# The gates stage of a diffusion trunk: a third hi/lo weight buffer, and every lo part on VectorE

## The reference

```python
def peer_ffn(h, w_q, keys, u_tab, v_tab):
    q = (h @ w_q)...                                   # 8 heads, two halves of 128
    s = jnp.einsum('bthcd,hckd->bthck', q, keys)       # 128 keys a half
    s_top, i_top = lax.top_k(s, PEER_TOPK)             # 16 of each half
    ...
    best_s, pos = lax.top_k(cand_s, PEER_TOPK)         # 16 of the 256 pairs
    idx = jnp.take_along_axis(cand_i, pos, axis=-1)    # experts out of 128 * 128
    gates = jax.nn.softmax(best_s, axis=-1)
    ...
    pre = jnp.einsum('ced,cd->ce', jnp.take(u_tab, ii, axis=0), hh)
    act = jax.nn.gelu(pre)
    return jnp.einsum('ce,ced->cd', act * gg, jnp.take(v_tab, ii, axis=0))
```

## Time and profile before

| | us |
|---|---|
| median of 3 runs | 4571.91 (4570.05 to 4576.68) |
| the profiled execution | 4570.1 |
| its span, first to last instruction | 4568.4 |
| gates stage, layer 0 | about 736 to 1616 of the span |
| gates stage, layer 1 | about 3279 to 3969 of the span |
| TensorE busy | 4062.0 (89%) |
| VectorE busy | 3121.7 (68%) |
| ScalarE busy | 1898.0 (42%) |
| GpSimd busy | 1492.6 (33%) |

### The profile page before, as it was taken

One profiled execution on the slowest core, in us unless ns is written; L12 is line 12 of the kernel. 1 busy time (PEld: TensorE's weight loads), 2 busy tenths in 40 slices (PEclk: granted clock), 3 DMA queues, 4 the chain that ended last, 5 costly groups with the idle time before them and its releaser, 6 DMA issues. The chain is left out here.

```text
span 4568.4 us, 62858 instructions
## 1 busy us (share of the span) xinstructions
PE 4062.0 (89%) x20380; PEld 3461.7 (76%) x20380; DVE 3121.7 (68%) x5714; ACT 1898.0 (42%) x3664; POOL 1492.6 (33%) x1048
## 2 busy tenths in 40 slices
PE   8687697899999989999978889867799999899998
PEld 2576586778888868888856767645699999899997
DVE  0675378998887668888874454534887765477777
ACT  1211222577777722222223333322257777533332
POOL 0122123555554434444412111102354444322221
PEclk9798898999999999999998898878899999899999
DMA  6333113799999999999941010011278888799996
GB/s 249 130 139 110 41 43 107 244 326 324 330 329 327 343 345 375 373 375 372 374 165 60 33 37 28 28 37 65 75 246 294 282 275 292 261 333 331 336 330 221
DMA packets 411875, 1025.96 MB, mean 225 GB/s; under 512 B 33968, under 2 KB 182448, under 8 KB 405680
## 3 DMA queue, kind: packets, MB, share of 16 engines
q1 hardware_dynamic: 301104, 621.00, 38.7%
q0 software_dynamic: 110592, 402.70, 24.6%
HBM read 904.03 MB, written 119.54 MB: 224 GB/s over the span
## 5 line engine op out<-in xcount | busy, mean ns | idle before, releaser
L156 PE MATMUL psum<-h_hi,w_hi 128*128 128x512 f32 (+1 forms) x2880 | 1140.1, 396 | 309.9 <-POOL w_lo L133 294.5
L129 ACT ACTIVATE w_hi<-w_raw 128x1024 fp32r<-128x1024 f32 x624 | 660.5, 1059 | 1471.1 <-PE psum L1215 863.0
L133 POOL TENSOR_TENSOR w_lo<-w_raw,w_hi 128x1024 fp32r<-128x1024 f32 x258 | 640.7, 2484 | 1471.2 <-ACT w_hi L129 1469.1
L157 PE MATMUL psum<-h_lo,w_hi 128*128 128x512 f32 (+1 forms) x2880 | 1095.4, 380 | 0.0
L158 PE MATMUL psum<-h_hi,w_lo 128*128 128x512 f32 (+1 forms) x2880 | 1094.9, 380 | 0.0
L156 PEld LDWEIGHTS psum<-h_hi,w_hi 128*128 128x128 f32 x2880 | 560.5, 195 | 396.1 <-POOL w_lo L133 188.6
L133 DVE TENSOR_TENSOR w_lo<-w_raw,w_hi 128x1024 fp32r<-128x1024 f32 x366 | 448.4, 1225 | 537.4 <-ACT w_hi L129 513.0
L1213 PE MATMUL psum<-a_hie,w_hi 128*128 128x512 f32 (+1 forms) x2048 | 758.9, 371 | 34.5 <-DVE a_loe L1266 34.5
L1214 PE MATMUL psum<-a_loe,w_hi 128*128 128x512 f32 (+1 forms) x2048 | 756.9, 370 | 0.0
L1215 PE MATMUL psum<-a_hie,w_lo 128*128 128x512 f32 (+1 forms) x2048 | 749.2, 366 | 0.0
L1198 POOL DMA_INDIRECT v_rowse<-in_peer_v,expert_idx x384 | 423.6, 1103 | 825.9 <-DVE row_sume L1275 812.8
(11 more groups left out here) (200 smaller groups left out, 4437.9 us busy)
## 6 DMA issues: line engine op xcount, KB each, us to landing
w_raw<-in_peer_u SPq DMA_DIRECT2D x256, 512.0 KB
w_raw<-in_peer_v SPq DMA_DIRECT2D x256, 512.0 KB
gates<-stageg SPq DMA_DIRECT2D x28, 2048.0 KB
acts<-act_gg SPq DMA_DIRECT2D x128, 256.0 KB
gte<-gates SPq DMA_DIRECT2D x32, 1024.0 KB
act_fe<-acts SPq DMA_DIRECT2D x128, 256.0 KB
ada_w<-in_ada_w SPq DMA_DIRECT2D x12, 2048.0 KB, 7.7
ada_rows<-in_ada_w SPq DMA_DIRECT2D x48, 512.0 KB, 3.5
```

The source lines that it names most:

```text
L129: act.activation(self.w_hi[:, s, :], self.raw[:, slot, :], ACT.Copy).then_inc(self.hi_done, 1)
L133: pool.tensor_tensor(self.w_lo[:, s, :], self.raw[:, slot, :], self.w_hi[:, s, :].bitcast(F32), ALU.subtract).then_inc(self.lo_done, 1)
L156: pe.matmul(out, wh, hi[:, k], start=(k == 0), stop=False)
L157: pe.matmul(out, wh, lo[:, k], start=False, stop=False)
```

## The change

The gates stage gets a third pair of hi and lo buffers, kept in a list `more` that only this stage fills. `W` = 3 is their number there, and tile c uses buffer c % 3. ScalarE makes the hi part of tile c+3 after product c, where it made that of tile c+2. VectorE makes all lo parts, tiles 0 and 1 before its first selection and then that of tile c+2 as it comes to tile c; GpSimd is left with the gathers. Room for the buffers comes from the gathered rows (`UBUF` 5 to 4) and the one-hots (`EQ` 3 to 2). The accumulators stay two, the raw slots four, and SP's loop isn't edited. GpSimd's list places each gather three tiles later than before, relative to the tiles that it no longer touches.

```diff
--- before.py
+++ after.py
@@ -44,7 +44,7 @@
 GROUPS = NKEYS // QUAD
 SPARSE = (2, 1)
 LEAD = (16, 20)
-UBUF = 5
+UBUF = 4
 VBUF = (8, 4)
 
 
@@ -96,6 +96,7 @@
         self.settled = sem("settled")
         self.tiles = 0
         self.wide = 2
+        self.more = []
 
     def sem(self, name):
 
@@ -119,19 +120,25 @@
         eng.sem_inc(self.settled, 1)
 
 
+    def weights(self, x):
+
+        if x < SPLIT:
+            return self.w_hi[:, x, :], self.w_lo[:, x, :]
+        return self.more[x - SPLIT]
+
     def load(self, sp, src, i, slot, n_raw, turn):
         sp.wait_ge(self.lo_done, i + (self.tiles + RAW - n_raw + 1))
         sp.dma_start(self.raw[:, slot, :], src).then_inc(self.raw_in[slot], 16)
 
     def hi(self, act, i, slot, s, turn):
         act.wait_ge(self.raw_in[slot], turn * 16 + (self.raw_at[slot] + 16))
-        act.wait_ge(self.tile_done, i + (self.tiles + 1))
-        act.activation(self.w_hi[:, s, :], self.raw[:, slot, :], ACT.Copy).then_inc(self.hi_done, 1)
+        act.wait_ge(self.tile_done, i + (self.tiles + 1 - len(self.more)))
+        act.activation(self.weights(s)[0], self.raw[:, slot, :], ACT.Copy).then_inc(self.hi_done, 1)
 
     def lo(self, pool, i, slot, s):
         pool.wait_ge(self.hi_done, i + (self.tiles + 1))
-        pool.tensor_tensor(self.w_lo[:, s, :], self.raw[:, slot, :], self.w_hi[:, s, :].bitcast(F32),
-                           ALU.subtract).then_inc(self.lo_done, 1)
+        hi, lo = self.weights(s)
+        pool.tensor_tensor(lo, self.raw[:, slot, :], hi.bitcast(F32), ALU.subtract).then_inc(self.lo_done, 1)
 
     def context_h(self, scope, tag):
 
@@ -143,14 +150,13 @@
         x = [(self.h_hi[:, :, 0:min(tokens, SEQ)], self.h_lo[:, :, 0:min(tokens, SEQ)])]
         return x + ([(self.hc_hi[:], self.hc_lo[:])] if tokens == TOK else [])
 
-    def product(self, pe, i, s, moving, ks=range(KC)):
+    def product(self, pe, i, s, moving, ks=range(KC), w=None):
 
         if ks[0] == 0:
             pe.wait_ge(self.lo_done, i + (self.tiles + RAW + 1))
             pe.wait_ge(self.acc_free[s], i // 2 + (self.tiles // 2 + 1))
         for k in ks:
-            wh = self.w_hi[:, s, k * P:(k + 1) * P]
-            wl = self.w_lo[:, s, k * P:(k + 1) * P]
+            wh, wl = (x[:, k * P:(k + 1) * P] for x in self.weights(s if w is None else w))
             for n, (hi, lo) in enumerate(moving):
                 out = self.psum[:, self.wide * s + n, 0:hi.shape[2]]
                 pe.matmul(out, wh, hi[:, k], start=(k == 0), stop=False)
@@ -773,7 +779,7 @@
     tag = f"g{layer}"
     K = TOPK
     STAGES, STAGE_G = P // STAGE_T, STAGE_T // 4
-    EQ, OJ = 3, 2
+    EQ, OJ, W = 2, 2, SPLIT + 1
     dots = S * P
     moving = t.moving(Td)
     t.wide = 1
@@ -797,6 +803,7 @@
         act_f = sb("act_g", [P, 2, Td])
         ubuf = sb("u_rows", [P, UBUF, D])
         pre_act = sb("pre_act", [P, S, P])
+        t.more = [(sb("w_hi", [P, D], F32R)[:], sb("w_lo", [P, D], F32R)[:])]
         h_row = t.psum[:, 2:4, :]
         gelu_done = t.sem("gelu_done" + tag)
         spilled = [t.sem(f"spilled{x}{tag}") for x in range(2)]
@@ -832,7 +839,7 @@
         turn_h = [next(p for p in range(END) if dots_by(p) >= P * s) for s in range(1, S)]
 
         def on_pool(c):
-            return c < lead or c % 2
+            return c < 0
 
         with nc.Block() as block:
 
@@ -848,9 +855,10 @@
                     dve.wait_ge(dv, steps[0])
 
                 def low(c):
+
                     if c < NKEYS and not on_pool(c):
                         dve.wait_ge(t.lo_done, c + (t.tiles + RAW))
-                        t.lo(dve, c, c % RAW, c % SPLIT)
+                        t.lo(dve, c, c % RAW, c % W)
 
                 def dots_to(upto):
 
@@ -893,7 +901,7 @@
                     while here[0] < min(upto, END):
                         p = here[0]
                         if p % KC == 0:
-                            low(p // KC + 1)
+                            low(p // KC + 2)
                         if p + 14 in group_at:
                             one_hots(group_at[p + 14])
                         if p % 2:
@@ -947,6 +955,8 @@
                         between()
                     return sparse
 
+                low(0)
+                low(1)
                 for n, (end, sparse, b) in enumerate(order):
                     begin, calls = here[0], [0]
 
@@ -1003,7 +1013,7 @@
                             turn(turn_at[p])
                         if p in group_at:
                             group(group_at[p])
-                        t.product(pe, c, c % SPLIT, moving, [k])
+                        t.product(pe, c, c % SPLIT, moving, [k], c % W)
 
             @block.scalar
             def _(act):
@@ -1014,8 +1024,8 @@
                 def ahead(c):
 
                     t.wait_product(act, c)
-                    if c + SPLIT < NKEYS:
-                        t.hi(act, c + SPLIT, (c + SPLIT) % RAW, c % SPLIT, (c + SPLIT) // RAW)
+                    if c + W < NKEYS:
+                        t.hi(act, c + W, (c + W) % RAW, c % W, (c + W) // RAW)
                     act.wait_ge(spilled[c % 2], 16 * (c // 2 + 1))
                     act.activation(act_f[:, c % 2], t.acc(c % SPLIT, Td), ACT.Gelu).then_inc(gelu_done, 1)
                     act.wait_ge(gelu_done, c + 1)
@@ -1051,7 +1061,7 @@
                         act.wait_ge(u_used, s * P)
                     act.activation(h_row, h_tok[:, s].rearrange("p (b n) -> p b n", b=2),
                                    ACT.Copy).then_inc(h_ready, 1)
-                for i in range(SPLIT):
+                for i in range(W):
                     t.hi(act, i, i, i, 0)
                 h_copy(0)
                 ends = [0] + [end for end, _, _ in order]
@@ -1081,8 +1091,8 @@
                 for c in range(NKEYS):
                     if on_pool(c):
                         pool.wait_ge(t.lo_done, c + (t.tiles + RAW))
-                        t.lo(pool, c, c % RAW, c % SPLIT)
-                    upto = dots if c == NKEYS - 1 else dots_by(c * KC) + UBUF
+                        t.lo(pool, c, c % RAW, c % W)
+                    upto = dots if c == NKEYS - 1 else dots_by((c - 3) * KC) + UBUF
                     if c * KC < lead * KC // 2 + 8:
                         upto = 0
                     while asked < min(dots, upto):
@@ -1125,7 +1135,7 @@
                 for x in range(2):
                     sp.wait_ge(spilled[x], 16 * (NKEYS // 2 + 1))
                     sp.wait_ge(stored[x], 16 * (n // 2 + 1))
-        t.wide = 2
+        t.wide, t.more = 2, []
         t.count_rows(dots, UBUF)
         t.end_stage(NKEYS, RAW)
```

## The result

The changed kernel takes 4909.62 us (median of 4 runs, 4902.97 to 4910.89), the kernel before 4570.98 on the same chip (4566.15 to 4576.68): a ratio of 1.0737 (95% interval 1.0719 to 1.0756), so 7.4% slower. Forecast were 4925 us and a range of 4700 to 5080. The profiled execution has a span of 4909.2 us against 4568.4, 340.8 more.

The account below looks back on a forecast made before the run. TensorE was taken to set the pace before, a one-tile load loop after; steady tiles 69 + 106, stores 90 + 61 and leads 15 + 10 made 351 us on 4570, given as 4925 us, range 4700 to 5080.

Parts of the forecast that it names:

- the two terms for steady tiles: Gates stage, steady tiles slowed by late loads: +69 us in layer 0, +106 us in layer 1.
- the other four: Terms for stores of gates, 90 and 61 us, and for the lead stretches, +15 and +10 us.
- The loop of one tile: Gelu, load issue, landing, hi part, next Gelu now span one tile, not two: 7.5 us in layer 0, 6.4 in layer 1.
- The landing: Time from a raw load's issue to its hi part: taken as 5.5 us in layer 0, 4.5 in layer 1.
- The 0.8 us for the activations: Part of the landing's lower bound: 256 KB of activations ahead in SP's queue add 0.8 us to 3.5.
- How a store costs: SP's load behind a gates store issues late and lands slower: 6 us a store in layer 0, 5.5 in layer 1.
- The leads: Lead stretches of the gates stage, where VectorE can't fit all lo parts: +15 and +10 us.
- The bound of 80 us: TensorE's waits for lo parts in both layers, without the starts: about 80 us, all the change can win.
- Only the stores bind: Rival: landings fall to their low end, layer 0 keeps TensorE's pace except at stores; 4710 us, chance 0.09.
- VectorE is the bound: Rival: loads are in time, VectorE's extra lo parts cost in leads and selections; 4600 us, chance 0.04.
- The smaller buffers: Four gathered-row slots and one-hots two deep cost nothing while the loop is the bound, else a few us.
- Faster: Rival: loads land within 4.4 us in layer 0, 3.2 in layer 1, and lo waits go; 4490 us, chance 0.05.

Follow-up runs that it names:

- run 1: Changed kernel with SP issuing the load of tile c+4 before it waits for Gelu c, not behind the activations of tile c; 4687.89 us.
- run 6: Changed kernel with one more load at the start and the load of tile c+5 behind the activations of tile c; 4577.46 us.
- run 7: Changed kernel with two more loads at the start and the load of tile c+6 behind the activations of tile c; 4523.68 us.
- run 10: Changed kernel with ScalarE doing the Gelu of product c ahead of the hi part of tile c+3, SP's loop unedited; 4803.30 us.
- run 2: Changed kernel with the load of tile c+4 still behind the wait for Gelu c, but issued ahead of the activations; 4876.04 us.
- run 3: Kernel before with all lo parts on VectorE and nothing else changed; 4586.74 us.
- run 8: Changed kernel with two more loads at the start, loads of tile c+6 behind activations c, and the lead's lo parts on GpSimd; 4506.98 us.
- Run 9: Kernel before with one more load at the start and the load of tile c+5 behind the activations of tile c; 4517.37 us.
- run 12: Changed kernel with two more loads at the start, loads of tile c+6 behind activations c, lead's lo parts on GpSimd, one-hots three deep; 4506.03 us.

## Why the prediction was right, point by point

The mechanism was right, and runs 1, 6, 7 and 10 show it. That the sum came within 6 us of the parts measured (351 forecast, 345) is partly luck: the two terms for steady tiles were too large by 20 and 29 us, the other four too small by 43 in all.

**The loop of one tile: right, and shown.** Its three terms were 1.0 and 0.9 us from Gelu to load (measured 0.98 and 0.88), 5.5 and 4.5 of landing to the hi part (5.51 and 4.61), and 1.0 from hi part to Gelu (0.96). The spacing was to be 7.5 and 6.4 us (7.47 and 6.44). Runs 1, 6 and 7 break the loop by asking sooner, run 10 by changing who stands behind the hi part; in all four the spacing falls.

**The landing: right value, partly by luck.** The 0.8 us for the activations ahead in the queue didn't exist (run 2). The load itself landed 5.2 us after its issue in layer 0 and 4.2 in layer 1 (medians), so what I put down to the activations is traffic beside the load: too much for the one and too little for the other made the right sum. By the Trainium skill (DMA: Bandwidth & Descriptors, Queues, rings and completion order) the engines take turns between queues packet by packet, from which I had estimated 6.7 us for loads always beside gathers. The packets in the trace are in line with that: of the 97 steady loads of layer 0 that don't follow a store, the 10 with gather packets in flight for over 95% of the landing took 6.2 us (median), the 14 with none 3.6, and on average gathers were beside a load for 53% of its landing.

**Steady tiles and stores: right in sum, off by up to a quarter in each.** Setting apart the gaps between Gelus above 10.5 us in layer 0 and 9.5 in layer 1: layer 0 has 18, of 229.6 us, and 93 others of 7.39 on average; layer 1 has 12, of 149.9, and 95 of 6.19. Over the 770.6 us of before, 111 x 7.39 is 49 (forecast 69), and the long gaps' surplus over 7.39 is 97 (90). In layer 1 it is 77 (106) and 76 (61). The long gaps average 12.8 and 12.5 us, where over 13 was forecast. The steady tiles are shorter than forecast because loads that don't follow a store landed in 5.1 and 4.2 us on average, for the 5.5 and 4.5 taken; in layer 1, 23 of 97 met no gather and landed in 3.5, which makes a tile of 5.4.

**How a store costs: the sum was right, the way to TensorE was not.** I had the load 4.5 us late in SP's queue and 1.3 us slower to land, 6 us a store in layer 0. Over its 15 stores the next load is issued 3.6 us after its Gelu on average, 2.7 late, and its hi part comes 8.4 us after that, 2.8 later than ordinary; SP's blocks behind stores shrank (the longest issue behind a store is 3.0 us on average, 6.8 before). Together that is 5.5. But the text named only the accumulator and SP's next load as what a late Gelu holds. In layer 0 most of TensorE's idle time comes another way: behind the late hi part ScalarE also has the scaled one-hots of the next group, 2.44 us, and that group stands ahead of the next matmuls in TensorE's order. These are the 125 us of line 1006: 114 of them fall in the 18 long gaps or just behind.

**The leads: mis-sized.** +15 and +10 were forecast, +17 and +29 measured. VectorE's lo parts are 8 and 6 us of it (run 3; 9 and 14 by runs 7 and 8); the rest is the load loop, which works in the lead too and goes in run 7 (105.8 and 104.6 us). The Trainium skill (Perfetto Trace Analysis, Optimizing Scalar/DVE Operations) says that when VectorE is saturated, moving some work off it, even to GpSimd, may make sense, but that between these two it might not help, as they share a read port. In the leads it did help: run 8 against run 7 puts 16.7 us on it.

**What the change can win.** The bound of 80 us stands, but its reading was too simple: those waits were put down to lo parts, and some 40 us of them were loads behind stores, which no third buffer helps. Run 9 wins them without one.

**The rivals.** "Only the stores bind" would have the loop vanish in layer 0: the hi part starts 0.07 us after the landing in most tiles, so no. "VectorE is the bound": no (run 3). The smaller buffers: the one-hots are free (run 12); four slots for rows weren't tried alone, but in the changed kernel VectorE waits 1.5 us for rows in all of layer 0. "Faster" needed loads inside 4.4 and 3.2 us: landings were 5.2 and 4.2.

**Left open.** What the lower clock (below) adds to the end, since the load loop hides part of it; and shared lo parts with a third buffer in layer 0.

## What to carry to other kernels

A buffer added in the middle of a chain moves the margin, it doesn't make one: what was asked for two products ahead is now asked for one ahead, unless the load is moved by as much. So find what issues the load, and count the instructions of the loop from that issue back to itself. Where a trace blames the last maker (a lo part), follow it back to the load before you give the maker more room; and issue a small load that others wait for ahead of a large store in the same queue, not behind it.

## What was not expected of the hardware

A stall costs TensorE more than its length. Around the store shown above, TensorE's timeline:

```profile
1103.57 0.39 PE L164 MATMUL psum<-h_hi,w_lo 128*128 128x512 f32 x1
1109.25 1.97 PE L1006 MATMUL psum<-ojg,eq_ig 128*128 128x128 f32 x8 [5.29 <-ACT ojg L1042]
...
1111.55 0.63 PE L163 MATMUL psum<-h_lo,w_hig 128*128 128x512 f32 x1
1111.97 0.63 PE L164 MATMUL psum<-h_hi,w_log 128*128 128x512 f32 x1
...
1113.62 0.39 PE L162 MATMUL psum<-h_hi,w_hig 128*128 128x512 f32 x1
1113.85 0.39 PE L163 MATMUL psum<-h_lo,w_hig 128*128 128x512 f32 x1
```

and the granted clock of the stretches (PEclk is the third figure from the end):

```profile
1100.00:1106.00 6.00, 3.96 (x18) 2.95 (x16) 1.94 (x4) 0.96 (x1) 1.88 (x2) 1.00 1.04 415
1106.00:1109.00 3.00, 0.00 (x0) 0.00 (x0) 2.80 (x7) 2.83 (x10) 0.00 (x0) 0.62 1.02 351
1109.00:1112.00 3.00, 2.75 (x11) 2.56 (x12) 2.96 (x16) 3.00 (x11) 0.00 (x0) 0.50 0.39 142
...
1115.00:1118.00 3.00, 3.00 (x19) 2.58 (x18) 3.00 (x6) 1.44 (x5) 1.21 (x2) 1.00 0.87 238
```

After 5.29 us without work the granted clock is 0.50, the 1.2 GHz level, and matmuls start 0.42 us apart; a few us later it is 1.00, the 2.4 GHz level, and they start 0.23 apart. Over the long stretches TensorE's busy time rose from 746.9 and 555.2 us to 793.0 and 600.9 for the same products. Read as "busy", 92 us of the loss would seem to be work.

The second surprise is the queue. In one queue 256 KB of activations ahead of a load cost its landing nothing that shows (run 2), while a 2 MB store ahead of it held the issue for 8.3 us on average in layer 0, and the data was used 16.4 us after the issue began, against 11.6 for the median load (run 1).
